# Seven two-part buffers moved to byte 64 of 256, and two transposes put behind each opening product

## The reference

```python
def swiglu(h, w1, w3, w2):
    return (jax.nn.silu(h @ w1) * (h @ w3)) @ w2
...
    h = h + g2 * swiglu(hn, ffn_w1[layer], ffn_w3[layer], ffn_w2[layer])      # blocks one and two, hidden 2816
...
        mix = jax.nn.sigmoid(gate_dn) * (o_dn @ w_proj_dn[l]) + jax.nn.sigmoid(gate_nsa) * (o_ns @ w_proj_nsa[l])
        x = x + mix @ w_out[l]
        h2 = rmsnorm(x, norm_mlp[l])
        x = x + jnp.square(jax.nn.relu(h2 @ w_up[l])) @ w_down[l]              # block three, hidden 4096
```

## The kernel before

| buffers | remainder before | remainder after |
|---|---|---|
| `whi`, `wlo` | 128 | 128 |
| `xh`, `xl` | 64 | 64 |
| `ah`, `al` | 0 | 64 |
| `xch`, `xcl` | 32 | 64 |
| `hh`, `hl` and `hh2`, `hl2` | 192 | 64 |
| `onh`, `onl` | 0 | 64 |
| `mxh`, `mxl`, `odh`, `odl` | 224 | 64 |

## Time and profile before

### The profile page before, as it was taken

The page is one execution under the profiler, slowest core; times in us unless marked ns, Lnnn a source line. Parts: engine busy times, 40 slices in busy tenths (PEclk is TensorE's granted clock), DMA queues, the critical chain, the costliest instruction groups (busy, mean ns, idle before and its releaser), DMA issues.

```text
span 1260.4 us, 24357 instructions
## 1 busy us (share of the span) xinstructions
PE 1184.9 (94%) x10454; PEld 1129.0 (90%) x10454; DVE 815.7 (65%) x1487; ACT 590.3 (47%) x1085; POOL 77.6 (6%) x94
## 2 busy tenths in 40 slices
PE   5888799999996999999979999998999999999999
PEld 1787699999986999999978888887998999999999
DVE  4764759988874676544453588887664665766543
ACT  2435545455444444543544466653224445555332
POOL 0000010000011000001000011112500001000000
PEclk9789999999997999999799899999999999999999
DMA  9660739988882557551254132220212454755520
GB/s 389 274 243 1 289 137 355 357 332 335 316 319 72 196 215 275 180 176 68 73 197 167 52 117 101 98 105 34 70 69 101 148 201 153 301 201 174 204 81 13
DMA packets 32363, 226.41 MB, mean 180 GB/s; under 512 B 3584, under 2 KB 4736, under 8 KB 5120
## 3 DMA queue, kind: packets, MB, share of 16 engines
q1 hardware_dynamic: 30528, 221.20, 47.1%
q10 hardware_dynamic: 1728, 3.67, 0.8%
HBM read 223.80 MB, written 1.05 MB: 178 GB/s over the span
## 4 chain that ended last, share of the span: by engine, by line
PE 82%; DVE 9%; ACT 5%; DMA 2%; issue 1%; POOL 0%; SPq 0%; DVEq 0%; ACTq 0%; POOLq 0%
PE bank L536 21%; PE bank L537 21%; PE bank L538 21%; DVE sb_wlo L1755 3%; ACT sb_whi L1285 2%; PE bank L972 2%; PE bank L634 1%; PE bank L564 1%; DVE sb_ring L1789 1%; DVE sb_tmp L1774 1%; DMA sb_ring<-in_f 1%; DMA sb_ring<-in_ada 1%; PE bank L574 1%; PE bank L554 1%; PE bank L994 1%; PE bank L963 1%
## 5 line engine op out<-in xcount | busy, mean ns | idle before, releaser
L536 PE MATMUL bank<-sb_xh,sb_whi 128*128 128x256 f32 x1496 | 427.9, 286 | 7.8 <-DVE sb_wlo L1755 5.6
L537 PE MATMUL bank<-sb_xl,sb_whi 128*128 128x256 f32 x1496 | 420.8, 281 | 0.0
L538 PE MATMUL bank<-sb_xh,sb_wlo 128*128 128x256 f32 x1496 | 420.8, 281 | 0.0
L1755 DVE TENSOR_TENSOR sb_wlo<-sb_ring,sb_whi 128x1024 fp32r<-128x1024 f32 (+1 forms) x201 | 244.2, 1221 | 142.0 <-ACT sb_whi L1285 141.3
L536 PEld LDWEIGHTS bank<-sb_xh,sb_whi 128*128 128x128 f32 x1496 | 286.8, 192 | 16.1 <-issue 12.6
L537 PEld LDWEIGHTS bank<-sb_xl,sb_whi 128*128 128x128 f32 x1496 | 286.3, 191 | 0.1
L538 PEld LDWEIGHTS bank<-sb_xh,sb_wlo 128*128 128x128 f32 x1496 | 284.9, 190 | 0.0
L1285 ACT ACTIVATE sb_whi<-sb_ring 128x1024 fp32r<-128x1024 f32 (+1 forms) x201 | 210.7, 1051 | 98.9 <-PE bank L538 87.4
L1755 DVE TENSOR_TENSOR sb_wlo<-sb_more,sb_whi 128x1024 fp32r<-128x1024 f32 x108 | 131.1, 1223 | 74.8 <-ACT sb_whi L1285 74.7
L537 PE MATMUL bank<-sb_hl,sb_whi 128*128 128x256 f32 x608 | 170.0, 280 | 0.0
L538 PE MATMUL bank<-sb_hh,sb_wlo 128*128 128x256 f32 x608 | 169.9, 279 | 0.0
(11 more groups left out here) (347 smaller groups left out, 1865.4 us busy)
## 6 DMA issues: line engine op xcount, KB each, us to landing
sb_more<-in_w SPq DMA_DIRECT2D x34, 1024.0 KB, 6.1
sb_ring<-in_w SPq DMA_DIRECT2D x32, 1024.0 KB, 5.7
sb_ring<-in_adaT SPq DMA_DIRECT2D x26, 1024.0 KB, 7.7
sb_ring<-in_f SPq DMA_DIRECT2D x24, 1024.0 KB, 5.0
sb_more<-in_adaT SPq DMA_DIRECT2D x18, 1024.0 KB, 9.0
sb_ring<-in_gn SPq DMA_DIRECT2D x8, 1024.0 KB, 4.8
sb_ring<-in_gd SPq DMA_DIRECT2D x8, 1024.0 KB, 4.9
sb_ring<-in_up SPq DMA_DIRECT2D x8, 1024.0 KB, 6.0
```

Of the source, the lines that this page charges most:

```text
L536: te.matmul(out, wh, rh, start=start, stop=False, skip_group_check=skip)
L537: te.matmul(out, wh, rl, start=False, stop=False, skip_group_check=skip)
L538: return te.matmul(out, wl, rh, start=False, stop=stop, skip_group_check=skip)
L1755: ve.tensor_tensor(lo, x, hi.bitcast(F32), ALU.subtract).then_inc(*lo_dve.up(n))
```

## The change

Six unused buffers, `gap`, are declared in front of two-part buffers so that these begin 64 bytes behind a multiple of 256 (table above). All buffers declared behind a gap in the same scope move with it; among them are `nq`, `ksw`, `vsw`, `ss`, `pt2`, `R1`, `Msb`, `SBs`, `more`, `z8`. Buffers declared in the outermost scope, the weights and `xh`, `xl`, `sq`, `con0` among them, stay. And a new helper, `pace`, issues two 128x128 transposes of the identity matrix into a bank of `RA` that nothing reads; `opening` calls it at its end.

```diff
+        def gap(n, size):
+
+            sb(f"gap{n}", [128, size // 4])
+
...
         qT = sb("qT", [128, 4, T])
+        gap(2, 64)
         ah = sb("ah", [128, 8, T], F32R)
...
         scope()
+        gap(3, 224)
         xch = sb("xch", [128, KT, T], F32R)
...
         scope()
+        gap(0, 128)
         hh = sb("hh", [128, NH0, T], F32R)
...
         qk = sb("qk", [128, 16, T])
+        gap(4, 64)
         onh = sb("onh", [128, 8, T], F32R)
...
         scope()
+        gap(5, 32)
         mxh = sb("mxh", [128, 8, T], F32R)
...
         more[2] = sb("more2", [128, NEXTRA, SLOT])
+        gap(1, 128)
         hh2 = sb("hh2", [128, NH2, T], F32R)
...
+            def pace():
+
+                ps = take(RA, ("idle", next(idles)))
+                for t in range(2):
+                    te.transpose(ps[:, t * 128:(t + 1) * 128], ident, ident)
...
                 for u in us:
                     F.done(u)
+                pace()
```

## The result

The median after is **1251.3 us** (1240.2 to 1255.8) against 1257.3 us before (1249.2 to 1266.6) in the same measurement: a ratio of 0.9948, with a 95% interval of 0.9924 to 0.9972. That is 6.0 us or half a per cent. The profiled execution took 1253.8 us, its span 1252.0 (1262.2 and 1260.4 before).

The account below looks back on a forecast made before the run. TensorE was taken as the bound, busy 94% of the span, through its step from pass to pass. From the profiled execution: 1262.2 - 7.7 - 8.2 - 1.7 + 0.7 = 1245.3, say 1245 us; 8-in-10 range 1239 to 1261.

Parts of the forecast that it names:

- the class that had most of the chance: Whole kernel: a time within 1% of the one before, given a chance of 0.58.
- each row draws its step: Rival on the up and down rows: turns decide nothing, steps drawn as before; about 1255 us, chance 0.25.
- Part 2: Down stages: buffers moved from byte 192 to 64 take over the up stage's step; 1824 passes, 8.2 us saved.
- addresses don't matter: Rival: the turns work but down stages are long for another reason; 1255 us, chance 0.12.
- Part 1: Second and third up stages: turns make them start at the short step; 4.5 and 3.2 us saved.
- Part 3: `ah`, `onh`, `odh`, `mxh` and partners: 768 passes get 2.2 ns shorter each, 1.7 us saved, bounds 0 and 5.1.
- Part 4: Turns at the three openings: each costs 0.23 us, 0.7 us added, with no waiting.
- The cover: First up and down stages: VectorE and DMA still keep up at the short step; down stage 0.85 and 0.89 busy.

Follow-up runs that it names:

- the second block above: Second block of a single run on the changed kernel: one turn and three turns alternately ahead of each up-stage product; whole run 1288.9 us.
- the kernel with more turns: Against the kernel with three turns at the openings: three turns also ahead of the `ah` row and the `odh` products; 1246.4 us, ratio 0.9913 to before.

## Why the prediction was right, and where it was not

The time lies in the range and in the class that had most of the chance, 6 us above the forecast and 4 below the middle of the rival "each row draws its step". The range takes in nearly all of that rival. So that the time fell into it does not bear out the forecast: the likeliest case is not what happened.

- **Part 2, the down stages: right.** They take the up stage's step: 113.3 behind 113.3 and 117.8 behind 117.8, in all 15 pairs of the five profiles with the gaps (the change, the gaps alone, and the three with three turns at the openings), of which one is long. In the three kernels with a piece ahead of every product the nine down stages took the step of the last product, five times the long one. In contrast, in the three profiles without gaps all nine down stages run at 117.8, behind either step. The rival "addresses don't matter" is out: the gaps alone give 7.7 us, ratio 0.9939.
- **Part 1, the up stages: this is the step that failed.** The prediction has "a fixed, unwaited piece ahead of it should decide it in the same way each time", and takes it to decide for the short step. Two turns do neither. In the profiles of this change and of the turns alone, the two openings that had ended in the long step were followed by a short row, the two that stood in the short step for many passes by a long one, and the two that had come to the short step a few passes behind a delay by a short one. Of the 7.7 us of this part the profiled execution got 3.1. Part 2 lost its 2.4 us of the second pair along with it.
- **Where the reasoning slipped.** The earlier trace rows show one place where two turns were followed by a short product. The product ahead of them stood in the short step too (steps of 113 to 114 ns up to 836.18), so it shows only that two turns can leave a short step as it is. It is the only such place in the kernel before. The step behind depends on the state ahead, and a piece shows its effect only in many places in a row.
- **The rival "each row draws its step"** came nearer for the turns: the turns alone give a ratio of 1.0004. It was wrong that it is a draw; the same piece in a row of products gives an exact period.
- **Part 3: near in size, by rows that the sum did not have.** `ah` and `mxh` went from 120 to 113.3, 1.3 us of passes each, and nothing of it reached the span: the sums behind these rows wait for the other engines (23.76 us before, 23.78 after). The sum priced the pass and did not look at what ends the row. What was gained, 2.9 us, came from `onh` and `odh` (0.9 and 2.0) with the 168 `xh` passes between the `odh` products, which the sum leaves out. `onh` had mostly stood at 118.8 before, not at 120. That 1.7 was near is luck.
- **Part 4: right for the turns.** From the last opening pass (194.59, one step behind 194.47) to the second pass behind the turns (195.05) are 0.46 us, as was said. The openings themselves took another 0.6 us (1.3 with the turns), which the sum does not have.
- **The cover: right.** In the first down stage VectorE is at 44.94 / 53 = 0.85 and DMA at 0.88, forecast 0.85 and 0.89, and TensorE is busy through all of it.
- **The rule of the Trainium skill** (page "TensorE: Matmul & The Clock Gate", Part 2, step-by-step: the moving operand and the weights come in through independent ports, so loading the next weights costs the running matmul nothing) was read in the prediction as leaving no room for an effect of the address. That reading fails here: with weights at the same place, the same sizes and order a pass took 113.3 ns with its buffers at byte 64, 117.8 at byte 192 and 120.0 at byte 128. Whether these nanoseconds come from the reading of the weights, which is all that the rule speaks of, no run here shows.

That the time came out high is thus in the main part 1, with what hangs on it: of the 8.5 us by which the profiled execution lies over 1245.3 the second pair is 6.9. With three turns in place of two the forecast's state, all six rows short, was reached: 1244.3 and 1247.9 us in two measurements, about the 1245 of the sum. Both are faster than the kernel before. Against the change only the first is clear of it (0.9841 to 0.9903 where the change has 0.9924 to 0.9972), and the two were not measured side by side.

What stays open is what it is that a piece moves. The runs show a state that outlasts a row, turns over with exact periods, and depends on which piece stands between; none shows what holds it, nor why three turns mostly end short. The openings with three turns were followed by a short row 12 times of 12 (by its last two steps the opening had ended long three times and short nine times), but 7 of 21 products in the second block above and the `odh` stage of the kernel with more turns were long behind three turns: a good habit and no proof. Nor does any run show why an address acts.

## What to carry to other kernels

Where long rows of passes run without a wait, work out the step from pass to pass per row, and compare rows that differ only in where their moving buffer begins; some padding may be worth 4% of such a row. Look at what the instruction behind the row waits for before you count the gain: two of the rows here got shorter passes and ended no sooner for the program. Try the address first by itself: its effect was there in every profile, while a filler ahead of a row works only by the state that it meets. And do not conclude from one place in a trace that a filler sets a state; put it ahead of many products, behind either state, and read the sequence.

## What the runs showed of the hardware

- The step of a 128x256 two-part pass depends on where the moving buffer begins, modulo 256 bytes (weights always at byte 128). Distance 192 for both parts: 113.3 or 117.8 ns. Distance 64: 117.8. Distance 0: 120.0. Distance 32: 116.7, behind a long row alone. Distance 224: 118.4. Distance 96: 120.0. Distance 128: 120.0 in one `ah` row and 118.7 in two, all ahead of the first turns. 16 bytes off 192: 119.2 and 119.3.
- At distance 192 there are two steady steps, 113.3 and 117.8, and a row of over 1500 passes stays in the one that it began with, across a change of operand. More than one step was seen at distance 128 as well.
- A fixed piece between products moves through the two with an exact period: three products for two turns, four for one turn, two for a float32 matmul of 256 columns, two for a pass of 128 columns, three for one of 64.
- The spread from run to run fits this in part: 17 us before and 16 after (20 runs each), 18 with the gaps alone and 9 with the turns alone (12 runs each), 6 and 7 in the two measurements of the kernel with three turns (6 and 7 runs), whose profiles have all six rows short, but 11 in the kernel with more turns (6 runs), whose profile has them short too. That it comes from the steps is not shown.
